# Keys and queries with tokens on the partitions, roots by token block, and a changed order of the attention loop

## Chip, cores and metric

One core of a Trainium2 chip. The time is device microseconds of one execution of the whole program; smaller is better. Engines: TensorE (PE, with its weight loads PEld), VectorE (DVE), ScalarE (ACT), GpSimd (POOL), and SyncE (SP), which issues the DMAs.

## The reference, cut to what matters

256 tokens of width 1024 pass two blocks in float32: six gated feed-forward networks, a mixer of four parts, a gated linear recurrence, and attention at the end. The change touches the keys and values, which come from one projection of the normalised activations, and the queries of the attention:

```python
def shared_kv(x, kv_gain, w_kv, k_gain):
    hkv = rms_norm_2(x, kv_gain)
    k, v = jnp.split(hkv @ w_kv, 2, axis=-1)
    return rms_norm_2(heads(k), k_gain), heads(v)          # 16 heads of 64

def stick_breaking_block(h, k, v, w_q, q_gain, w_o):
    q = rms_norm_2(heads(h @ w_q), q_gain)
    o = stick_breaking_attention(q, k, v)                   # two blocks of 128 queries
    ...
    # z = q k / 8;  w[t, s] = sigmoid(z[t, s]) * prod over s' in (s, t) of sigmoid(-z[t, s']);  o = w v
```

`rms_norm_2` divides by the root of the mean square plus 1e-6 and multiplies by a gain. Keys and queries are thus normalised twice: the input over 1024 features of a token, the result over the 64 features of a head.

## The kernel before, in words

Activations lie with features on the partitions: `x` is 128 x 8 tiles x 256 tokens. Every float32 weight block (128 x 1024, 512 KB) is loaded by SP into one of six slots of `raw`; ACT copies it to `w_hi` in the type fp32r (`hi`, L652), and POOL, or DVE for some blocks, subtracts that from `raw` and gives `w_lo` (`lo`, L557, L1072). The activations are cut likewise into a high and a low half (`xn`, and `kv_in` for the keys and values). A product is then three: high by high, high by low, low by high. All engines go through the blocks in one order; a slot is free for `raw` after `lo_ready`, and for `w_hi` after `used`, which TensorE raises at a block's last product.

The stages that matter are `kv` (8 blocks of keys `split_in`, 8 of values `split_rows`), the feed-forward `ffn_e`, then `q_in` (8 blocks `split_in`), the attention, and `attn_out` (8 blocks of rows, the first two used in float32 without cutting).

Keys and queries before: `projections` makes a tile of 128 output features by 256 tokens at a time, with the weights loaded into the array and 256 tokens moving (`head_tiles`, L1861 to L1863). The first four tiles run together, input tile by input tile, and `total_squares` (L1893) sums the squares of x over the features in between. DVE multiplies each tile by `rstd` out of PSUM (`take`, L1278), ACT squares two tiles at a time (L957).

- For the keys, a product with `head_ones` (L2378, 128x512) sums the squares over the features of a head, ACT takes the root (L962), DVE the reciprocal of 128x512 (L1702) and the scaled product (L1703). The values have tokens on the partitions (`rows_tile`, L1958 to L1960: tokens loaded, 512 weight columns moving) and need `rstd` as a column: four records of L2389.
- For the queries, the squares are summed with tokens on the partitions (`token_squares`, L2415), ACT takes roots of 8 or 16 columns (L990), DVE their reciprocals (L1746), and `over_features` (L2427) spreads them over 64 partitions each by products with the identity; DVE then scales (L1751).

The attention loop runs over eight pairs of heads `c`. For each: `logits` on PE (L2441 to L2447) into banks 0 to 3, two sigmoids on ACT (L1008), a recurrence along the keys (L1767) and the product that gives the weights on DVE (L1771), six transposes on PE into banks 4 and 5 (L2499), their copy by ACT (L1024), `weighted_values` on PE (L2459 to L2463), and their copy to `y` (L1013). `rows(0)` and `rows(1)` (L1923) start the output projection in float32; they write banks 0 to 3, and so wait for the last sigmoids. `unused_products(2)` are two products (L2474) whose result is not used.

Each engine's instructions run in the order written. The waits are on counters: `need(engine, name, value)` waits until the counter has that value.

## Time and profile before

| | us |
|---|---|
| median of 3 runs | 1542.15 (1541.9 to 1542.18) |
| the profiled execution, time | 1542.68 |
| the profiled execution, span | 1540.5 |
| PE busy | 1526.4 (99%) |
| DVE busy | 1070.8 (70%) |
| POOL busy | 925.2 (60%) |
| ACT busy | 777.9 (50%) |
| chain that ended last, PE | 92% |
| HBM read, mean | 261 MB, 170 GB/s |
| granted TensorE clock, tenths | 9, the highest digit, in all 40 slices |

The busy time of PE is from each matmul's start to its modelled end, and these overlap: what one costs in a full stream is the distance between the starts of neighbours. In a timeline row the first number is the start from the span's beginning, the second the length, and `xN` the number of records merged into the row. A float32 matmul leaves two records, one in fp32r or a transpose leaves one. Where an engine idled before a row, the row says for how long and what ended it.

### The profile page before, as it was taken

How to read it: one execution, taken by the hardware profiler on the slowest of the kernel's cores; microseconds unless marked ns; L12 is line 12 of the kernel's file. 1: busy time of each engine (PE TensorE's matmuls, PEld its weight loads, DVE VectorE, ACT ScalarE, POOL GpSimd, SP SyncE). 2: the span in 40 equal slices, each digit the busy share in tenths (PEclk: the TensorE clock that was granted, in tenths of full speed). 3: DMA queues.
4: the chain of work that ended last, by engine and by line, in shares of the span. 5: the costliest groups of instructions: out<-in, count | busy, mean ns of one | idle time of the engine just before them, and what ended most of it. 6: DMA issues, size and time to landing. Idle time of an engine off the chain costs nothing.

```text
span 1540.5 us, 25103 instructions
## 1 busy us (share of the span) xinstructions
PE 1526.4 (99%) x9754; PEld 1332.9 (87%) x9754; DVE 1070.8 (70%) x1475; ACT 777.9 (50%) x1119; POOL 925.2 (60%) x1092
## 2 busy tenths in 40 slices
PE   9999999999999999999999999999999999999998
PEld 7888888887888888888999888888888889888887
DVE  7866555765976668976589976657866655697664
ACT  6554432023654565554666654555555455665542
POOL 4966520201686677876776686677967671167663
PEclk9999999999999999999999999999999999999999
DMA  8666533232656565665635566564565562346653
GB/s 299 207 198 182 192 110 110 70 97 83 204 197 194 164 200 163 198 199 183 200 124 186 182 197 194 165 225 145 179 201 180 171 221 67 125 164 204 184 162 119
DMA packets 107350, 263.69 MB, mean 171 GB/s; under 512 B 9184, under 2 KB 43104, under 8 KB 107104
## 3 DMA queue, kind: packets, MB, share of 16 engines
q1 hardware_dynamic: 107232, 262.09, 52.5%
q8 instruction: 78, 1.28, 0.3%
q14 instruction: 40, 0.33, 0.1%
HBM read 261.00 MB, written 1.05 MB: 170 GB/s over the span
## 4 chain that ended last, share of the span: by engine, by line
PE 92%; DVE 5%; ACT 1%; DMA 1%; issue 1%; POOL 0%; SPq 0%; DVEq 0%; ACTq 0%
PE ps L1827 42%; PE ps L1828 24%; PE ps L1877 6%; PE ps L1830 5%; PE ps L1923 2%; PE ps L1861 2%; PE ps L1863 2%; PE ps L1862 2%; PE ps L1944 1%; PE ps L2135 1%; DMA raw<-blocks 1%; PE ps L2030 1%; DVE arena L1767 1%; PE ps L1960 0%; PE ps L1958 0%
## 5 line engine op out<-in xcount | busy, mean ns | idle before, releaser
L557 POOL TENSOR_TENSOR w_lo<-raw,w_hi 128x256 fp32r<-128x256 f32 x1056 | 904.4, 889 | 494.9 <-ACT w_hi L652 491.2
L1827 PE MATMUL ps<-xn,w_hi 128*128 128x512 f32 x1848 | 660.1, 396 | 1.3 <-DVE xn L1083 0.7
L652 ACT ACTIVATE w_hi<-raw 128x1024 fp32r<-128x1024 f32 (+1 forms) x517 | 476.8, 933 | 187.3 <-PE ps L1830 104.3
L1828 PE MATMUL ps<-xn,w_lo 128*128 128x256 f32 x2112 | 550.4, 280 | 0.0
L1827 PEld LDWEIGHTS ps<-xn,w_hi 128*128 128x128 f32 x1848 | 346.5, 187 | 77.9 <-DVE xn L1083 1.4
L1828 PEld LDWEIGHTS ps<-xn,w_lo 128*128 128x128 f32 x2112 | 398.4, 189 | 17.4
L1827 PE MATMUL ps<-hid,w_hi 128*128 128x512 f32 x1008 | 363.5, 397 | 0.0
L1072 DVE TENSOR_TENSOR w_lo<-raw,w_hi 128x512 fp32r<-128x512 f32 (+1 forms) x246 | 285.8, 1163 | 39.2 <-ACT w_hi L652 34.2
L1828 PE MATMUL ps<-hid,w_lo 128*128 128x256 f32 x1056 | 292.5, 282 | 0.0
L1827 PEld LDWEIGHTS ps<-hid,w_hi 128*128 128x128 f32 x1008 | 190.2, 189 | 41.0
L1178 DVE TENSOR_TENSOR arena<-ps,low_part 128x512 f32<-128x512 f32 x132 | 90.8, 688 | 191.6 <-ACT low_part L767 191.4
L1828 PEld LDWEIGHTS ps<-hid,w_lo 128*128 128x128 f32 x1056 | 198.5, 188 | 7.5
L767 ACT ACTIVATE low_part<-ps 128x512 f32<-128x512 f32 x132 | 78.3, 593 | 172.6 <-PE ps L1830 172.5
L772 ACT ACTIVATE arena<-arena 128x256 f32<-128x256 f32 x132 | 55.3, 419 | 147.0 <-DVE arena L1188 147.0
L1188 DVE TENSOR_TENSOR arena<-arena,rstd 128x512 f32<-128x512 f32 x132 | 111.8, 847 | 4.5
L1830 PE MATMUL ps<-xn,w_hi 128*128 128x512 f32 x264 | 104.1, 396 | 0.0
L1877 PE MATMUL ps<-xs,raw 128*128 128x256 f32 x432 | 98.3, 382 | 0.0
L1198 DVE TENSOR_TENSOR h<-arena 128x256 f32<-128x256 f32 x132 | 93.2, 706 | 0.0
L1877 PEld LDWEIGHTS ps<-xs,raw 128*128 128x128 f32 x432 | 80.7, 190 | 12.2 <-issue 1.1
L1199 DVE TENSOR_TENSOR hid<-h,hid 128x256 fp32r<-128x256 f32 x132 | 86.6, 656 | 4.5
L1197 DVE TENSOR_TENSOR hid<-arena 128x256 fp32r<-128x256 f32 x132 | 61.2, 464 | 29.1 <-ACT arena L772 29.1
L1220 DVE SCALAR_TENSOR_TENSOR x<-ps,x 128x512 f32<-128x512 f32 x24 | 16.5, 686 | 73.1 <-PE ps L1830 73.1
(342 smaller groups left out, 1490.3 us busy)
## 6 DMA issues: line engine op xcount, KB each, us to landing
raw<-blocks SPq DMA_DIRECT2D x418, 512.0 KB, 3.6
raw<-blocks SPq DMA_DIRECT2D x146, 256.0 KB, 3.5
cst<-consts SPq DMA_DIRECT2D x1, 2358.0 KB, 14.3
x<-x_in SPq DMA_DIRECT2D x4, 256.0 KB, 5.5
out<-x SPq DMA_DIRECT2D x4, 256.0 KB, 3.3
cst<-consts SPq DMA_DIRECT2D x1, 109.0 KB, 2.1
```

Of the source, the lines that this page charges most:

```text
L557: ins = nc.gpsimd.tensor_tensor(w_lo[:, slot(n), piece], raw[:, slot(n), piece], w_hi[:, slot(n), piece], ALU.subtract)
L652: nc.scalar.activation(w_hi[:, slot(n), cols], raw[:, slot(n), cols], ACT.Copy)\
L767: nc.scalar.activation(low_part[:, :, :], ps[:, b:b + 2, SEQ:], ACT.Copy).then_inc(low_taken, 1)
L1072: nc.vector.tensor_tensor(w_lo[:, slot(n), cols], raw[:, slot(n), cols], w_hi[:, slot(n), cols], ALU.subtract).then_inc(lo_ready[slot(n)], 1)
L1178: nc.vector.tensor_tensor(gate_up[:, :, :], ps[:, b:b + 2, 0:SEQ], low_part[:, :, :], ALU.add)\
L1188: nc.vector.tensor_tensor(gate_up[:, :, :], gate_up[:, :, :], over(rstd[:, :], 2), ALU.mult)\
L1198: chain(nc.vector.tensor_tensor(h[:, :], gate_up[:, 1, :], gs, ALU.mult))
L1199: nc.vector.tensor_tensor(hid[:, c, 1, :], h[:, :], hid[:, c, 0, :], ALU.subtract)\
L1827: nc.tensor.matmul(where, hi, both.rearrange("p a t -> p (a t)"), start=opens, stop=False)
L1828: ins = nc.tensor.matmul(where[:, 0:SEQ], lo, high, start=False, stop=False)
L1830: ins = nc.tensor.matmul(where, hi, both.rearrange("p a t -> p (a t)"), start=False, stop=True)
L1877: ins = nc.tensor.matmul(where, raw[:, slot(n), k * P:k * P + P], xs[:, k, :], start=k == 0, stop=k == KD - 1)
```

## The change

The 16 blocks of key and query weights are loaded in another cut (`split_cols`): a block holds two input tiles for four output tiles, in four pieces of 256 columns. `token_steps` loads 128 tokens of the activations into the array and moves 512 weight columns, two input tiles a block; the first half (output tiles 0 to 3) is complete before the second, in banks 4 and 5, then 6 and 7. The norm over the 1024 features is not applied to keys and queries: since q/rstd cancels under the second norm but for epsilon, the mean square of a head gets the bias 1e-6 times (mean square of x plus 1e-6), `heads_eps`. Per half `u` (0 and 1 keys, 2 and 3 queries) and block of 128 tokens `t`: ACT squares 128x512 out of PSUM, DVE sums groups of 64 (`tensor_reduce`), ACT takes 8 roots, DVE 8 reciprocals and the product 128x512, PE turns it with four transposes (`turn`) in the same bank, and ACT or DVE copy it with the gain into `k_t` or `q_t`. `total_squares` is replaced in these stages by `token_totals`, after step 7 of 8 of the first half; `rstd` over features is kept for `ffn_e` alone. `head_ones` products, `token_squares`, `over_features`, the column products and `unused_products` go. In the loop the sigmoids of pair 2 stand ahead of the first copy of weights, and the row tiles 0 to 7 of `rows(0)` come as (0, 1), (2, 3, 4), (5, 6, 7), the first two before the transposes of pair 6; they were (0 to 3) after its values and (4 to 7) after the transposes of pair 7.

```diff
--- before.py
+++ after.py
@@ -116,9 +116,9 @@
...
-    add("kv", ["split_in"] * 8 + ["split_rows"] * 8)
+    add("kv", ["split_cols"] * 8 + ["split_rows"] * 8)
...
-    add("q_in", ["split_in"] * 8)
+    add("q_in", ["split_cols"] * 8)
...
+        def token_bank(half, t):
+
+            return 4 + 2 * half + t
+
+        def token_tiles(b):
+
+            return ps[:, b, :].rearrange("p (o m) -> p o m", m=P)
...
+                elif KINDS[n] == "split_cols":
+                    start, cols = h0 + 4 * (at // 4), slice(PAIR * (at % 4), PAIR * (at % 4) + PAIR)
+                    sp.dma_start(raw[:, slot(n), :].rearrange("p (o m) -> p o m", m=PAIR),
+                                 blocks[start:start + 4, :, cols].rearrange("o p m -> p o m")).then_inc(arrived[slot(n)], 16)
...
+                if gains in TOKEN_NORMS:
+                    return
...
+            def heads_square(u, n0):
+
+                last = n0 + 4 * (u % 2) + 3
+                act.wait_ge(used[slot(last)], nth(last))
+                for t in range(TB):
+                    nc.scalar.activation(sq_heads[2 * (u % 2) + t], ps[:, token_bank(u % 2, t), :], ACT.Square)\
+                        .then_inc(ev["heads_sq"], 1)
+
+            def heads_root(u):
+                for t in range(TB):
+                    need(act, "heads_sums", 2 * u + t + 1)
+                    nc.scalar.activation(heads_inv[:, u % 2, t, :], heads_inv[:, u % 2, t, :], ACT.Sqrt, scale=1.0 / HD,
+                                         bias=heads_eps[:, t:t + 1]).then_inc(ev["heads_root"], 1)
+
+            def heads_take(u, t, dst, by):
+
+                need(act, "heads_turned", 2 * u + t + 1)
+                half = u % 2
+                nc.scalar.activation(dst[:, 4 * half:4 * half + 4, t * P:t * P + P], token_tiles(token_bank(half, t)), ACT.Copy,
+                                     scale=const(by)).then_inc(ev["heads_ready"], 1)
...
-                for a in range(4):
-                    heads_square(1, a)
-                    hi_until(n0 + 9 + a)
-                for a in range(4):
-                    heads_root(1, a)
-                    hi_until(n0 + 13 + a)
+                act.wait_ge(total_ready, state["norms"])
+                nc.scalar.activation(rstd_col[:, :], ps[:, 3, SEQ:SEQ + TB], ACT.Sqrt, scale=1.0 / D, bias=const("norm_eps"))
+                nc.scalar.activation(rms[:, :], ps[:, 3, 0:SEQ], ACT.Sqrt, scale=1.0 / D, bias=const("norm_eps"))\
+                    .then_inc(rms_ready, 1)
+                heads_square(0, n0)
+                hi_until(n0 + 9)
+                heads_root(0)
+                hi_until(n0 + 12)
+                for t in range(TB):
+                    heads_take(0, t, k_t, "k_norm")
+                hi_until(n0 + 13)
+                heads_square(1, n0)
+                hi_until(n0 + 14)
+                heads_root(1)
+                hi_until(n0 + 16)
+                for t in range(TB):
+                    heads_take(1, t, k_t, "k_norm")
                 hi_until(n0 + 2 * KD + 4)
                 act.wait_ge(used[slot(n0 + 2 * KD - 1)], nth(n0 + 2 * KD - 1))
-                need(act, "col_out", 1)
+                act.wait_ge(rstd_ready, state["norms"])
                 for t in range(TB):
                     ins = nc.scalar.activation(v_heads[:, t, :], ps[:, 2 * t:2 * t + 2, :].rearrange("p b s -> p (b s)"),
                                                ACT.Copy, scale=rstd_col[:, t:t + 1])
                 ins.then_inc(ev["v_out"], 1)
...
+                n0, out_rows = FIRST["q_in"], FIRST["attn_out"]
+                hi_until(n0 + KD - 1)
+                heads_square(2, n0)
+                heads_root(2)
                 preload(ACT.Sigmoid)
                 need(act, "at_mask", 1)
...
+                def take_weights(c):
                     need(act, "at_wt", c + 1)
                     nc.scalar.activation(weights_t[c % 2][:, :, :].rearrange("p (b m) s -> p b (m s)", b=2),
                                          ps[:, 4:6, 0:3 * P], ACT.Copy).then_inc(ev["at_wt_out"], 1)
+
+                heads_take(2, 0, q_t, "q_norm")
+                sigmoids(0)
+                sigmoids(1)
+                preload(ACT.Sqrt)
+                heads_square(3, n0)
+                heads_root(3)
+                preload(ACT.Sigmoid)
+                sigmoids(2)
+                take_weights(0)
+                heads_take(3, 0, q_t, "q_norm")
+                for c in range(1, KD):
+                    if c + 2 < KD:
+                        sigmoids(c + 2)
+                    take_weights(c)
                     if c == KD - 1:
                         hi_until(out_rows + 4)
-                    if c:
-                        output(c - 1)
+                    output(c - 1)
                     if c == KD - 2:
                         hi_until(out_rows + 3)
...
+                if gains and gains not in TOKEN_NORMS:
                     inverse_root(gains)
+
+            def token_norm(gains):
+
+                norms[0] += 1
+                v.wait_ge(total_ready, norms[0])
+                return nc.vector.tensor_scalar(heads_eps[:, :], ps[:, 3, SEQ:SEQ + TB], NORM_EPS / D, NORM_EPS * NORM_EPS, ALU.mult, ALU.add)
...
+            def heads_sums(u):
+
+                for t in range(TB):
+                    need(v, "heads_sq", 2 * u + t + 1)
+                    signal(nc.vector.tensor_reduce(heads_inv[:, u % 2, t, :], sq_heads[2 * (u % 2) + t].rearrange("p (g s) -> p g s", s=HD),
+                                                   axis=mybir.AxisListType.X, op=ALU.add), "heads_sums")
+
+            def heads_unit(u):
+
+                half = u % 2
+                for t in range(TB):
+                    inv = heads_inv[:, half, t, :]
+                    need(v, "heads_root", 2 * u + t + 1)
+                    chain(nc.vector.reciprocal(inv, inv))
+                    by = heads_inv[:, half, t, :].unsqueeze(2).broadcast_to([P, 8, HD])
+                    signal(tt(heads_tok[:, t, HALF * half:HALF * half + HALF].rearrange("p (g s) -> p g s", s=HD),
+                              ps[:, token_bank(half, t), :].rearrange("p (g s) -> p g s", s=HD), by, ALU.mult), "heads_unit")
+
+            def heads_take(u, t, dst, by):
+
+                need(v, "heads_turned", 2 * u + t + 1)
+                half = u % 2
+                tsc(dst[:, 4 * half:4 * half + 4, t * P:t * P + P], token_tiles(token_bank(half, t)), const(by), None, ALU.mult)\
+                    .then_inc(ev["heads_ready"], 1)
...
-                heads_take(n0, 0)
-                heads_take(n0, 1)
                 for a in range(4):
                     low_halves("g_ffn_e", a)
+                roots[0] += 1
+                v.wait_ge(rms_ready, roots[0])
+                chain(token_norm("g_kv"))
+                nc.vector.reciprocal(rstd_col[:, :], rstd_col[:, :]).then_inc(rstd_ready, 1)
+                heads_sums(0)
+                heads_unit(0)
+                chain(nc.vector.reciprocal(rstd[:, :], rms[:, :]))
                 lo(n0 + 9)
-
-                need(v, "col_done", 1)
-                signal(nc.vector.tensor_copy(rstd_col[:, :], ps[:, 3, 0:TB]), "col_out")
-                heads_take(n0, 2)
-                heads_take(n0, 3)
+                heads_sums(1)
+                heads_unit(1)
                 lo(n0 + 13)
-                for a in range(4):
-                    heads_finish(1, a, k_t, "k_norm")
...
+                token_norm("g_attn").then_inc(rstd_ready, 1)
+                v.wait_ge(rstd_ready, norms[0])
+                heads_sums(2)
+                heads_unit(2)
+                heads_take(2, 1, q_t, "q_norm")
                 for c in range(KD):
-                    if c == 1:
-                        take_query(7)
-                        scaled_queries(2)
+                    if c == 2:
+                        heads_sums(3)
+                        heads_unit(3)
+                        heads_take(3, 1, q_t, "q_norm")
...
+            def token_totals(over_features=False):
+
+                norms[0] += 1
+                pe.wait_ge(sum_ready, norms[0])
+                if over_features:
+                    mm(ps[:, 3, 0:SEQ], const("all_ones"), squares_sum[:, 0:SEQ], start=True, stop=True)
+                for t in range(TB):
+                    ins = mm(ps[:, 3, SEQ + t:SEQ + t + 1], squares_sum[:, t * P:t * P + P], const("all_ones")[:, 0:1], start=True, stop=True)
+                ins.then_inc(total_ready, 1)
+
+            def token_steps(n0, halves, half, steps, after_norm=None):
+
+                for k in steps:
+                    n = n0 + 4 * half + k // 2
+                    if after_norm is not None:
+                        pe.wait_ge(xn_lo_ready, KD * SPLIT_NORMS.index(after_norm) + k + 1)
+                    if k % 2 == 0:
+                        pe.wait_ge(lo_ready[slot(n)], nth_split(n))
+                    wh, wl = (w[:, slot(n), :].rearrange("p (o k m) -> p k o m", k=2, m=P)[:, k % 2] for w in (w_hi, w_lo))
+                    for t in range(TB):
+                        where, tok = token_tiles(token_bank(half, t)), slice(t * P, t * P + P)
+                        mm(where, halves[:, k, 0, tok], wh, start=k == 0, stop=False)
+                        mm(where, halves[:, k, 0, tok], wl, start=False, stop=False)
+                        ins = mm(where, halves[:, k, 1, tok], wh, start=False, stop=k == KD - 1)
+                    if k % 2:
+                        ins.then_inc(used[slot(n)], 1)
+
+            def turn(u, t):
+
+                need(pe, "heads_unit", 2 * u + t + 1)
+                half = u % 2
+                for i in range(4):
+                    at = HALF * half + i * P
+                    ins = nc.tensor.transpose(ps[:, token_bank(half, t), i * P:i * P + P], heads_tok[:, t, at:at + P], const("ident"))
+                ins.then_inc(ev["heads_turned"], 1)
...
+                token_steps(n0, kv_in, 0, range(7), "g_kv")
+                token_totals(over_features=True)
+                token_steps(n0, kv_in, 0, (7,), "g_kv")
+                token_steps(n0, kv_in, 1, range(6))
+                turn(0, 0)
+                turn(0, 1)
+                token_steps(n0, kv_in, 1, (6, 7))
                 pe.wait_ge(rstd_ready, norms[0])
-                for t in range(TB):
-                    ins = mm(ps[:, 3, t:t + 1], rstd[0:1, t * P:t * P + P], const("all_ones")[0:1, 0:1], start=True, stop=True)
-                ins.then_inc(ev["col_done"], 1)
-                tile(2)
-                need(pe, "col_out", 1)
-
-                need(pe, "proj_out", before + 6)
                 for k in range(KD):
                     rows_tile(n0 + KD + k, kv_in[:, k, :, :], start=k == 0, stop=k == KD - 1)
-                    if 1 <= k < 5:
-
-                        need(pe, "proj_out", before + KD)
-                        heads_squares(1, k - 1)
+                    if k == 2:
+                        turn(1, 0)
+                        turn(1, 1)
+                need(pe, "heads_ready", 4)
...
-                    if c == 0:
-                        need(pe, "proj_out", before + 6)
+                    need(pe, "heads_ready", 6 if c < 4 else 8)
                     if c == 1:
-                        need(pe, "q_root", 2)
+                        pe.wait_ge(rstd_ready, norms[0])
                     if c >= 2:
                         need(pe, "at_sig", c - 1)
...
                     if c < 2:
-                        need(pe, "heads_ready", 4 + 3 + c)
+                        need(pe, "heads_ready", 8)
...
+                token_steps(n0, xn, 0, range(7), "g_attn")
+                token_totals()
+                token_steps(n0, xn, 0, (7,), "g_attn")
+                token_steps(n0, xn, 1, range(3))
+                turn(2, 0)
+                turn(2, 1)
+                token_steps(n0, xn, 1, (3,))
+                logits(0)
+                token_steps(n0, xn, 1, (4,))
+                logits(1)
+                token_steps(n0, xn, 1, (5, 6, 7))
+                logits(2)
+                turn_weights(0)
+                logits(3)
+                turn(3, 0)
+                turn(3, 1)
+                for c in range(1, KD):
+                    if c == KD - 2:
+                        rows(0, (0, 1))
+                    turn_weights(c)
+                    if c == KD - 1:
+                        rows(0, (5, 6, 7))
+                    weighted_values(c - 1)
+                    if c == KD - 2:
+                        rows(0, (2, 3, 4))
                     if c == 1:
-                        over_features(3)
-                    if c == KD - 1:
-                        rows(0, range(4, KD))
-                    if c:
-                        weighted_values(c - 1)
-                    if c == KD - 2:
-                        rows(0, range(4))
+                        logits(4)
                     if c + 4 < KD:
                         logits(c + 4)
                 rows(1, range(4))
```

## Rows read from the trace of the kernel before

**Rows 1.** The page's first part: busy time, share of the span, instructions.
```profile
PE 1526.4 (99%) x9754; PEld 1332.9 (87%) x9754; DVE 1070.8 (70%) x1475; ACT 777.9 (50%) x1119; POOL 925.2 (60%) x1092
```

**Rows 2.** Timeline of PE, key-and-value stage: start us, us, engine, line, operation, shape, count.
```profile
1033.32 0.28 PE L1861 MATMUL ps<-kv_in,w_hi 128*128 128x256 f32 x1
...
1039.07 0.59 PE L1893 MATMUL ps<-arena,cst 128*128 128x256 f32 x2
...
1039.62 0.28 PE L1862 MATMUL ps<-kv_in,w_hi 128*128 128x256 f32 x1
...
1062.97 1.02 PE L2378 MATMUL ps<-arena,cst 128*128 128x512 f32 x2
...
1064.06 0.40 PE L1959 MATMUL ps<-w_lo,kv_in 128*128 128x512 f32 x1
...
1076.03 0.39 PE L1958 MATMUL ps<-w_hi,kv_in 128*128 128x512 f32 x1
...
1082.83 0.39 PE L1827 MATMUL ps<-xn,w_hi 128*128 128x512 f32 x1
```

**Rows 3.** Timeline of PE, query projection with its sums and spreads.
```profile
1274.17 0.59 PE L1893 MATMUL ps<-arena,cst 128*128 128x256 f32 x2
...
1283.23 1.84 PE L2415 MATMUL ps<-cst,arena 128*128 128x2 f32 x16
...
1285.14 0.28 PE L1862 MATMUL ps<-xn,w_hi 128*128 128x256 f32 x1
...
1287.98 1.97 PE L2427 MATMUL ps<-cst,q_inv 128*64 128x128 f32 x32
...
1290.10 0.28 PE L1862 MATMUL ps<-xn,w_hi 128*128 128x256 f32 x1
```

**Rows 4.** Timeline of PE, logits, turned weights, values and row tiles.
```profile
1295.01 0.70 PE L2441 MATMUL ps<-arena 64*128 64x256 f32 x4
...
1296.21 0.28 PE L1861 MATMUL ps<-xn,w_hi 128*128 128x256 f32 x1
...
1324.80 0.82 PE L2499 MATMUL ps<-cst,arena 128*128 128x128 f32 x6
1325.46 1.89 PE L1923 MATMUL ps<-y,raw 128*128 128x256 f32 x8
1327.28 0.44 PE L2459 MATMUL ps<-arena 128*64 128x128 f32 x4
...
1328.09 1.99 PE L1923 MATMUL ps<-y,raw 128*128 128x256 f32 x8
```

**Rows 5.** Windows: stretch, its length, busy us of each engine, granted clock, DMA.
```profile
1057.50:1082.80 25.30, 25.30 (x106) 19.55 (x105) 17.25 (x9) 12.03 (x14) 20.35 (x28) 1.00 0.53 177
1268.40:1304.70 36.30, 36.03 (x320) 34.28 (x319) 20.68 (x38) 17.12 (x26) 9.28 (x14) 1.00 0.28 84
1304.70:1325.50 20.80, 18.61 (x186) 15.35 (x185) 18.11 (x14) 18.11 (x27) 0.00 (x0) 1.00 0.01 2
```

**Rows 6.** Timeline of ACT, attention: a table load, two pairs' sigmoids, one copy of weights.
```profile
1294.12 1.28 ACT L663 ACT_TABLE_LOAD   x1
...
1295.65 2.92 ACT L1008 ACTIVATE arena<-ps 128x768 f32<-128x768 f32 x4
...
1305.93 0.82 ACT L1024 ACTIVATE arena<-ps 128x768 f32<-128x768 f32 x1
```

**Rows 7.** Timeline of DVE: reciprocal, two-input sum, small reciprocal, recurrence, weights.
```profile
1066.91 3.35 DVE L1702 RECIPROCAL arena<-arena 128x512 f32<-128x512 f32 x1
...
1272.69 0.68 DVE L1095 TENSOR_TENSOR arena<-arena,xs 128x512 f32<-128x512 f32 x1
...
1294.20 0.20 DVE L1746 RECIPROCAL q_inv<-q_inv 128x8 f32<-128x8 f32 x1 [0.66 <-ACT q_inv L990]
...
1315.73 1.77 DVE L1767 TENSOR_TENSOR_SCAN arena<-arena 128x774 f32<-128x774 f32 x1
1317.54 0.96 DVE L1771 TENSOR_TENSOR arena<-arena 128x768 f32<-128x768 f32 x1
```

## What the change should do to the time

> **What bounds the kernel now.** Read the page's first part first: TensorE is busy in 99% of the span [rows 1]. In such a kernel a microsecond counts only if it is TensorE's, as work or as idle time. Then the timeline of PE, where the distance of starts gives the real price of a product. In the key stage 48 products of 256 columns lie between 1033.32 and 1039.07: 0.120 us each. From 1076.03 to 1082.83 there are 30 products of 512 columns: 0.227 each [rows 2]. Last the windows, for idle time. In the query stage PE misses 0.27 us of 36.30, and in the loop 2.19 of 20.80 [rows 5], so there a second bound is close. DVE's recurrence starts at 1315.73, its weights product at 1317.54 for 0.96 us, and the next recurrence follows at about 1318.53 [rows 7]: 2.8 us a pair, back to back.
>
> **The key stage.** It runs from 1033.32 to 1082.83, 49.5 us [rows 2]. Its parts:
> - 192 products of 256 columns at 0.120: 23.0. After: 96 of 512 at 0.227, 21.8. Columns are equal, seams are fewer.
> - Totals: 1039.62 less 1039.07 less one product of 0.12, 0.43. After: the same 0.43 and two products of one moving column. Eight such products (16 records) took 1285.14 − 1283.23 − 0.12 = 1.79 [rows 3], 0.22 each; together 0.87.
> - Values, 96 of 512 columns: 21.8, before and after.
> - Four `head_ones` products: 1064.06 − 1062.97 − 0.23 = 0.86 each [rows 2], 3.4. They go.
> - The rest, 49.5 − 23.0 − 0.43 − 21.8 − 3.4 = 0.9, is the column products and seams; I keep 0.3 of it.
> - New: 16 transposes. Six took 1325.46 − 1324.80 = 0.66 [rows 4], 0.11 each, 1.8.
>
> After: 21.8 + 0.87 + 21.8 + 1.8 + 0.3 = 46.6, **2.9 us less**, if nothing waits. Count from the stage's start. Half 0 ends at 11.8. ACT still has the halves for `ffn_e` and two roots in front of its squares and starts them about 13.3; I take 0.68 for each 128x512 operation on ACT or DVE (the sum of two inputs, [rows 7]) and 0.20 for each one on 8 columns (the small reciprocal, [rows 7]). Squares, sums, one copy of a weight block, roots and products come to about 18; the turn stands at 19.9. For half 1: squares from 24, product done by about 30, turn at about 31.7. Both have some 2 us to spare. The moves on the queues: on ACT, squares, roots and takes stand ahead of later `hi` copies, so `w_hi` of the next blocks, then POOL's low halves, then SP's loads, queue behind them. But blocks now come free one by one (each 12 x 0.227 = 2.7 us) where four were released together, and ACT stands idle over half of the value stretch, POOL 5 of 25 us [rows 5]. DVE loses four reciprocals of 3.35 us there [rows 7]. I cost the queues at nothing; should cover fail, one copy of about 1 us stands ahead of a block.
>
> **The query stage and the loop.** The start is 1274.17 less 48 x 0.12 = 1268.42 [rows 3]; all times from here count from it. The last transposes (pair 7) start at 1324.80, that is 56.4 [rows 4]. TensorE's work loses 1.2 in the projection, 32 records of `token_squares` (2 x 1.79 = 3.6), 64 of `over_features` (2 x (1290.10 − 1287.98 − 0.12) = 4.0 [rows 3]) and two unused products (2 x 0.43); it gains 1.8 of transposes: 7.9 net. Whether that reaches the end depends on the chains of ACT and DVE, so I lay the order out:
> - PE: seven steps of 6 x 0.227 = 1.36 to 9.5, totals to 10.0, half 0 done at 11.3, three more steps to 15.4.
> - ACT squares 11.6 to 12.9; DVE sums to 13.7, products done at 14.5 and 15.4. `turn(2, 0)` at 15.4 is just met, `turn(2, 1)` at 15.9 too. ACT's table load of 1.28 [rows 6] fits before the take at 16.1. Copies done at 17.2.
> - Logits 0 at 17.7, at 1.2 each (1295.01 to 1296.21 [rows 4]), a step, logits 1, three steps to 25.7. ACT's sigmoids, 2.92 / 4 = 0.73 each [rows 6], give pair 0 at 20.7, pair 1 at 23.2; DVE's weights are ready at 23.6 and 26.4.
> - PE goes on: logits 2 to 26.9, transposes 0, logits 3 to 29.0. ACT loads the root table and squares from 25.9 to 27.3; DVE sums, behind its second weights, to 28.0; products at 28.9 and 29.8. `turn(3, 1)` waits about 0.4, done at 30.4.
> - ACT: table load, sigmoids 2 from 29.8 to 31.3, copy of weights 0 (0.82 [rows 6]) to 32.1. The transposes of pair 1 need banks 4 and 5 and wait for that copy: a **new stall of 1.7 us**, behind it on PE the values and logits 4 and 5.
> - DVE: recurrence 2 from 31.4 (37.7 before); six pairs of 2.8 end at 48.3, the last sigmoids at 45.4. PE's first two row tiles wait for these (about 0.6 idle), then 2 x 0.43 (eight records of L1923 from 1325.46 to 1327.28 are four tiles, 0.45 each), transposes 0.7, values 0.8 (1327.28 to 1328.09 [rows 4]), three tiles 1.3: transposes 7 at 49.1.
>
> Before they stood at 56.4 with four tiles done, now at 49.1 with five: 7.3 + 0.45 = **7.7 us less**. The tail behind (rows, values, `output_rows`) is unchanged on PE, and its `hi` and `lo` of output blocks keep their distance. Bounds: if the stalls vanished, DVE would still allow transposes 7 at 47.4 at the earliest, a gain of 9.4. For `tensor_reduce` of 128x512 no row exists; below lies 0.2 (eight elements), above 3.35 (the slowest DVE operation on that shape [rows 7]). I take 0.68, the other one-pass operation. The moving operand in four runs has no row either: the ends are 0.227, all in one run, and 0.43 for 256 columns in float32; I take 0.227, since nothing but the addresses differs from the value stretch.
>
> A page speaks against the sums on DVE: by the Trainium skill, VectorE: DVE Perf Modes, section Rules for kernel authors, a tensor_reduce on the hot path never leaves the single-rate mode and is called the slowest operation; its table's single-rate float32 figure, scaled to 512 columns, is an estimate of 0.57 us, with which the sum stays as it is. On the strided weights the Trainium skill, SBUF — State Buffer, section Door 1: The DMA port swizzle, charges each step to a new 16-byte line, and runs of 128 floats touch as many lines as one run does; by that the price is the contiguous one.
>
> **Sum.** 2.9 + 7.7 = 10.6 from the profiled execution's 1542.68 gives 1532.1; that execution lies 0.5 above the median, so 1531.5 as a median.
>
> **The rivals.**
> - *The gain is partly turned into waits* (chance 0.17): the turns are met with only 0.1 to 0.4 us, and each 0.3 more on a square, sum or product delays both query halves and the loop behind. Two units late by 1 us each, and 1 to 2 us more where copies wait on ACT: 3 to 5 us lost, 1534.5 to 1537. For it: the tight turns, and ACT and DVE each busy 18.1 of 20.8 us in the loop [rows 5]. Against: DVE waits in the query stage (20.7 busy of 36.3).
> - *The moving operand in four runs is slower* (0.04): the place is `token_steps`, 192 products; each 0.1 us more costs 19 us. It decides from 10.6 / 192 = 0.055, that is at 0.28 a product. At the float32 end, 0.86 for 512 columns, it would be 120 us; at 0.34, midway to the 0.45 of half rate, 1553. Slower. Against: the float32 columns of the head are read in the same way from the same array.
> - *A slow sum over groups* (0.03): at 3.35 each, two sums stand in each query half, 5 us late twice, and the key turns miss their 2 us by 3 twice: 10 to 16 lost of the 10.6 gained, 1541.5 to 1547: no change or slower.
> - *The clock is granted lower* (0.02): with stalls of 1.7 us and many transposes PE might fall to 1.2 GHz; 10 us of such work would cost 10, so no change. Against: 1.00 in the loop, with 2.19 us idle [rows 5].
> - *Nothing of it happens* (0.02): the stages keep their length because transposes in a bank just read, or loads in 1 KB pieces, hold PE; 1542.
>
> My forecast has 0.72. **Predicted 1531.5 us.** The range takes in the vanished stalls (9.4 + 2.9 = 12.3, 1529.8, and a little for the seams) and the first rival: 1529 to 1537. About 0.2% (3 us) is what a measurement can tell from no change; faster by that 0.90, within it 0.05, slower 0.05.
>
> **What would show it.** L1861 to L1863 gone from both stages and in their place 512-column products at 0.227; the key stage 46.6 long; transposes 7 at 49 from the query start; PE idle near 1.7 before the transposes of pair 1, released by ACT's copy; recurrences 2 to 7 back to back at 2.8. A distance above 0.25 in the new products, or a PE wait over 1 us at a turn for DVE, would make the prediction wrong.

## The result, and the profile after

The changed kernel takes 1532.16 us (median of 4 runs, 1531.4 to 1533.08) against 1542.16 before (1541.9 to 1542.41): ratio 0.9935, interval 0.9918 to 0.9953. It is faster by 0.65%, and the prediction of 1531.5 is 0.7 us off. The profiled execution took 1531.62, with a span of 1529.6; the span before was 1540.5, so the traces differ by 10.9 us.

The first part of the page of the changed kernel (share of the span and instructions; beside [rows 1], 10.2 us of TensorE's work and 266 matmul records are gone):

```profile
span 1529.6 us, 24560 instructions
PE 1516.2 (99%) x9488; PEld 1316.1 (86%) x9488; DVE 1047.1 (68%) x1471; ACT 779.6 (51%) x1127; POOL 919.8 (60%) x1092
```

Its PE timeline in the key stage, from the first key product to the first product of `ffn_e` (start, length, line, shapes, records):

```profile
1032.93 0.40 PE L2428 MATMUL ps<-w_hi,kv_in 128*128 128x512 f32 x1
...
1049.77 0.39 PE L2429 MATMUL ps<-w_lo,kv_in 128*128 128x512 f32 x1
...
1052.71 0.39 PE L2430 MATMUL ps<-w_hi,kv_in 128*128 128x512 f32 x1
1052.94 1.03 PE L2440 MATMUL ps<-cst,arena 128*128 128x128 f32 x8
1053.73 0.48 PE L2428 MATMUL ps<-w_hi,kv_in 128*128 128x512 f32 x1
...
1064.73 1.03 PE L2440 MATMUL ps<-cst,arena 128*128 128x128 f32 x8
1065.52 0.48 PE L1992 MATMUL ps<-w_hi,kv_in 128*128 128x512 f32 x1
...
1079.23 0.39 PE L1861 MATMUL ps<-xn,w_hi 128*128 128x512 f32 x1
```

L2428 to L2430 are the new products, with 512 weight columns moving; L2440 is the turn of keys or queries. From 1049.77 to 1052.71 there are 13 products, 0.226 us each. Each eight transposes cost 0.79 to 0.80 (1052.94 to 1053.73), without a wait before them. The stage lasts 1079.23 − 1032.93 = 46.30; it was 49.51 [rows 2].

DVE in the changed kernel, the keys' first half (L1739 sums over groups, L1748 small reciprocals, L1750 scaled products):

```profile
1046.23 1.39 DVE L1739 TENSOR_REDUCE heads_inv<-arena 128x8 f32<-128x512 f32 x2
1047.65 0.20 DVE L1748 RECIPROCAL heads_inv<-heads_inv 128x8 f32<-128x8 f32 x1
1047.89 0.69 DVE L1750 TENSOR_TENSOR arena<-ps,heads_inv 128x512 f32<-128x512 f32 x1
...
1048.85 0.69 DVE L1750 TENSOR_TENSOR arena<-ps,heads_inv 128x512 f32<-128x512 f32 x1
```

Two sums take 1.39, 0.70 each, about as much as the scaled product beside them. The products are done at 1049.54; the turn that reads them stands at 1052.94, so 3.4 us are in hand.

PE in the changed kernel, from the query stage's first product to the end of the loop. L2508 are the six transposes of a pair's weights, L1957 the row tiles (two records a tile):

```profile
1264.83 0.40 PE L2428 MATMUL ps<-w_hi,xn 128*128 128x512 f32 x1
...
1295.00 0.66 PE L2440 MATMUL ps<-cst,arena 128*128 128x128 f32 x4 [0.31 <-DVE arena L1750]
1297.26 0.85 PE L2508 MATMUL ps<-cst,arena 128*128 128x128 f32 x6 [1.60 <-ACT arena L1045]
...
1308.65 0.85 PE L2508 MATMUL ps<-cst,arena 128*128 128x128 f32 x6 [0.18 <-ACT arena L1045]
...
1310.36 1.13 PE L1957 MATMUL ps<-y,raw 128*128 128x256 f32 x4
...
1312.89 1.56 PE L1957 MATMUL ps<-y,raw 128*128 128x256 f32 x6
1314.29 0.82 PE L2508 MATMUL ps<-cst,arena 128*128 128x128 f32 x6
...
1339.08 0.50 PE L1861 MATMUL ps<-xn,w_hi 128*128 128x512 f32 x1
```

From here on times count from the query stage's first product. The turn of the last queries waits 0.31 us. The transposes of pair 1 wait 1.60 us, released by L1045, ACT's copy of weights 0: the predicted new stall. The transposes of pair 7 start at 49.46, with five tiles in front of them; before at 56.38 with four [rows 3, 4]. The first product of `ffn_f` (the last row) comes at 74.25; before it came at 81.61, so the query stage with all up to `ffn_f` is 7.36 shorter.

ACT in the changed kernel, ahead of that stall (L982 roots, L677 the table of the sigmoids, L1036 sigmoids of pair 2, L1045 the copy):

```profile
1293.05 0.30 ACT L982 ACTIVATE heads_inv<-heads_inv,heads_eps 128x8 f32<-128x8 f32 x1 [0.42 <-DVE heads_inv L1739]
1293.37 1.28 ACT L677 ACT_TABLE_LOAD   x1
1294.66 0.20 ACT L677 ACTIVATE table<-table 1x4 f32<-1x4 f32 x1
1294.90 1.51 ACT L1036 ACTIVATE arena<-ps 128x768 f32<-128x768 f32 x2
1296.30 0.82 ACT L1045 ACTIVATE arena<-ps 128x768 f32<-128x768 f32 x1
```

ACT is busy from 1293.05 to the end of the copy at 1297.12: root, table, sigmoids and copy run one after the other, and PE, idle from 1295.66, waits for the last of them. The windows of the changed kernel (busy us of PE, PEld, DVE, ACT, POOL, then the clock) show how full the loop is:

```profile
1264.83:1294.00 29.17, 29.17 (x155) 23.39 (x153) 20.70 (x35) 16.58 (x26) 10.25 (x14) 1.00 0.30 104
1294.00:1316.00 22.00, 19.86 (x178) 15.97 (x178) 19.52 (x17) 20.14 (x32) 0.00 (x0) 1.00 0.01 2
1316.00:1339.10 23.10, 23.10 (x187) 21.58 (x186) 12.79 (x17) 13.03 (x21) 6.80 (x8) 1.00 0.65 242
```

The idle time of PE in the query stage, 2.14 us, all lies in the middle window; it was 0.27 + 2.19 before [rows 5], and nothing behind these windows. So of the 7.36 us, 7.04 are removed work and 0.32 less idling, and the stall of 1.60 took the place of waits that were there already. The balance of the two traces: 3.21 + 7.36 = 10.57, and 0.39 from an earlier start of the key stage; together 10.96 of 10.9. The 0.39 is no part of the change: TensorE's code in front is the same in all kernels, and over the profiles of this document the stage starts anywhere from 1032.35 to 1033.73. `ffn_e`, between the two stages, lasts 185.60 after and 185.59 before.

### The profile page after: what moved, and what is told of

Same layout as the page of the kernel before. It is cut to its first block, busy times and chain, and to the rows that moved or that the text cites. A ratio compares the mean times of both kernels' runs of the same rounds, so it can differ in the third digit from the quotient of the medians.

```text
span 1529.6 us, 24560 instructions
## 1 busy us (share of the span) xinstructions
PE 1516.2 (99%) x9488; PEld 1316.1 (86%) x9488; DVE 1047.1 (68%) x1471; ACT 779.6 (51%) x1127; POOL 919.8 (60%) x1092
## 3 DMA queue, kind: packets, MB, share of 16 engines
q8 instruction: 75, 1.23, 0.3%
## 4 chain that ended last, share of the span: by engine, by line
PE 92%; DVE 4%; ACT 1%; DMA 1%; issue 1%; POOL 0%; SPq 0%; DVEq 0%; ACTq 0%
PE ps L1861 42%; PE ps L1862 24%; PE ps L1911 6%; PE ps L1864 5%; PE ps L1957 2%; PE ps L1978 1%; PE ps L2428 1%; PE ps L2430 1%; PE ps L2429 1%; PE ps L2169 1%; PE ps L2064 1%; DMA raw<-blocks 1%; PE ps L1897 1%; PE ps L1896 1%; PE ps L1895 1%
```

## The experiments

Every kernel is a variant of the changed one. "Key stage", "transposes 7" and "to `ffn_f`" are read as above: 46.30, 49.46 and 74.25 in the changed kernel; 49.51, 56.38 and 81.61 before.

**The keys alone.** The queries are computed and normalised as before, and the attention loop has its old order (the diff shows a part of the edit).

```diff
-    add("q_in", ["split_cols"] * 8)
+    add("q_in", ["split_in"] * 8)
...
-TOKEN_NORMS = ("g_kv", "g_attn")
+TOKEN_NORMS = ("g_kv",)
...
-                heads_square(2, n0)
-                heads_root(2)
+                pair_square(0)
+                pair_square(1)
+                token_roots(0, 1)
+                pair_square(2)
+                token_roots(2, 2)
```

> The key-and-value stage is as in the changed kernel, the query stage and the attention loop are those of before. Theory (two independent gains): about 3.2 us below the kernel before (49.5 us less the 46.3 that the trace of the changed kernel shows for this stage), 1539.0, and a ratio near 0.998; the key stage 46.3 long in the trace, the time from the query start to the transposes of pair 7 again 56.4. Rival (the two stages share a resource, for instance POOL's lead at ffn_e, so that the key stage alone gives other than its share): under 1.5 or over 5 us. On the spread of the changed kernel's times (1531.4 to 1533.1, mean granted clock 0.998 in the slower ones): if the attention's new order brings it, this kernel's times lie within 0.5 us and its clocks are 1.000; if the key stage brings it, they spread by 1.5.

Measured: 1538.63 (11 runs, 1538.14 to 1539.37) against 1541.87 (15 runs), ratio 0.9978, interval 0.9969 to 0.9987. Key stage 46.30, transposes 7 at 56.25, to `ffn_f` 81.48. The last sentence of the expectation was not met on either side: the times spread by 1.23 us and yet all granted clocks are 0.999 or 1.000. The 15 times of the kernel before spread by 1.56 us, with the same clocks. So a spread of this size is no sign of the clock by itself.

**The changed kernel again**, on the same chip, unedited.

> The changed kernel once more, nothing edited. Theory: 1531.4 to 1533.1 as before, ratio 0.993 to 0.994; the slower times are those with a mean granted clock below 1.000, 0.75 us for each 0.001 (half clock over 1.5 us). Rival (the spread is another thing): times and clocks are not in one order.

Measured: 1531.65 (1531.23, 1531.61, 1531.65, 1532.64, 1532.66), ratio 0.9935, interval 0.9922 to 0.9947. So the two parts come apart on one chip: the keys give 1541.87 − 1538.63 = 3.24, the queries with the new order of the loop 1538.63 − 1531.65 = 6.98. The traces say 3.21 and 7.36. The five times fall into two groups 1 us apart; what that is comes below. The price in the expectation is too low by half: 0.001 of the mean clock is 1.5 us of a span of 1530, not 0.75.

**Weights in one run.** The moving operand of `token_steps` is read in one run of 512 instead of four of 128. The kernel leaves out the choice of the right columns: its keys and queries are other numbers, with products of the same count and shape.

```diff
-                    wh, wl = (w[:, slot(n), :].rearrange("p (o k m) -> p k o m", k=2, m=P)[:, k % 2] for w in (w_hi, w_lo))
+                    wh, wl = (w[:, slot(n), HALF * (k % 2):HALF * (k % 2) + HALF] for w in (w_hi, w_lo))
...
-                        where, tok = token_tiles(token_bank(half, t)), slice(t * P, t * P + P)
+                        where, tok = ps[:, token_bank(half, t), :], slice(t * P, t * P + P)
```

> token_steps reads its 512 weight columns as one run of the block in place of four runs of 128; keys and queries are then other numbers. Theory (four runs cost nothing): 0.227 us a product as in the changed kernel, and the time is unchanged within 0.5 us. Rival (each jump of address costs a few ns that the modelled ends hide): below 0.225 a product, and 192 products give 1 us or more.

Measured: 1531.57; key stage 46.3, transposes 7 at 49.46, to `ffn_f` 74.25, all as in the changed kernel. Its PE groups of the keys' products (records, busy us, mean ns):

```profile
L2428 PE MATMUL ps<-w_hi,kv_in 128*128 128x512 f32 x32 | 12.7, 396 | 0.0
L2430 PE MATMUL ps<-w_hi,kv_in 128*128 128x512 f32 x32 | 12.5, 390 | 0.0
L2429 PE MATMUL ps<-w_lo,kv_in 128*128 128x512 f32 x32 | 12.5, 390 | 0.0
```

The changed kernel's groups of the same lines have the same numbers, 396, 390 and 390 ns. Four runs cost nothing that these traces show; that rival is excluded, not only unlikely.

**Sums of the queries' first half twice.** The spare time of the query turns, priced: one more `tensor_reduce` for each token block of `heads_sums(2)`.

```diff
                     need(v, "heads_sq", 2 * u + t + 1)
+                    for _ in range(1 if u in (2,) else 0):
+                        chain(nc.vector.tensor_reduce(heads_inv[:, u % 2, t, :], ...))
```

> Each of the two sums over groups of the first query half is done twice (0.7 us more each), result unchanged. Theory (the first query turn has 0.1 to 0.3 us of slack, and what is behind it is shifted whole): PE waits about 1.2 us before the second block's turn, and transposes 7 stand 1.1 to 1.3 us later from the query start, 50.7. Rival (slack downstream, the 1.6 us stall before the transposes of pair 1, swallows it): transposes 7 stay within 0.4 us of 49.5 and that stall shrinks.

Measured: 1533.43 (span 1531.5), transposes 0 of the loop at 28.35 instead of 27.11, transposes 7 at 50.70, to `ffn_f` 75.49. Its PE timeline at the two query turns:

```profile
1281.67 0.66 PE L2443 MATMUL ps<-cst,arena 128*128 128x128 f32 x4 [0.51 <-DVE arena L1753]
1282.63 0.66 PE L2443 MATMUL ps<-cst,arena 128*128 128x128 f32 x4 [0.30 <-DVE arena L1753]
```

About 1.4 us of added DVE work arrive as 1.24 us at the end, as expected, but the wait is not the one of 1.2 us that was expected: it is 0.51 before the first turn and 0.30 before the second, the rest longer distances beside them. The query turns have almost nothing in hand, as the layout said ("just met"), and nothing behind absorbs it: the stall before the transposes of pair 1 is 1.61 here too.

**Sums of the keys four times.**

```diff
                     need(v, "heads_sq", 2 * u + t + 1)
+                    for _ in range(3 if u in (0, 1) else 0):
+                        chain(nc.vector.tensor_reduce(heads_inv[:, u % 2, t, :], ...))
```

> Each sum over groups of the keys is done four times (three more of 0.7 us, 4.2 us more in each half), result unchanged. In the changed kernel the products of the keys are done 3.4 us and 1.9 us ahead of the end of their turns' natural start. Theory (slack is what the trace shows, and only the excess costs): the first half's second turn waits about 0.45 us, the second half's about 0.8, the key stage is 47.4 to 47.8 long in place of 46.3, the query stage is unchanged. Rival (DVE's delayed low halves of blocks 9 and 13, or SP's loads behind them, hold PE too): a wait of PE for w_lo or a key stage over 49.

Measured: 1534.46 (span 1532.6), key stage 47.92. That is 0.12 above the expected range. Its PE timeline shows waits at the key turns, for DVE's products (idle before, in brackets):

```profile
1053.79 0.66 PE L2443 MATMUL ps<-cst,arena 128*128 128x128 f32 x4 [0.31 <-DVE arena L1753]
...
1065.62 0.66 PE L2443 MATMUL ps<-cst,arena 128*128 128x128 f32 x4 [0.27 <-DVE arena L1753]
1066.59 0.66 PE L2443 MATMUL ps<-cst,arena 128*128 128x128 f32 x4 [0.30 <-DVE arena L1753]
```

Six added sums of 0.70, 4.2 us of DVE a half, cost the key stage 1.62 in all: 0.88 in these three waits, the rest in longer distances around them (the four transposes from 1052.83 to 1053.79, without their wait, take 0.65 where four in a full stream take 0.40). So most of the added work was absorbed: the slack of 3.4 and 1.9 us at the turns was real. By it, one more sum a block (1.4 us a half) should have been free in the key stage, where it cost 1.24 in the query stage; that kernel was not run.

This trace had something that I had not expected of it: to `ffn_f` 75.73, 1.48 more, in a stage that the edit does not touch. One of its windows (columns as above; clock after the five engines):

```profile
1298.50:1302.00 3.50, 3.25 (x20) 2.62 (x22) 3.43 (x3) 3.00 (x6) 0.00 (x0) 0.51 0.01 2
```

From 1298.5 to 1302.0 the granted clock is 0.51 on average, the level of 1.2 GHz; cut finer, it is 0.50 from 1298.6 to 1302.0 and 1.00 on both sides. The fall begins within the stall of pair 1, on this kernel's PE timeline 1.61 us:

```profile
1298.75 1.51 PE L2511 MATMUL ps<-cst,arena 128*128 128x128 f32 x6 [1.61 <-ACT arena L1045]
1300.19 0.70 PE L2492 MATMUL ps<-arena 128*64 128x128 f32 x4
```

Six transposes take 1.51 where they took 0.85. In the trace of the changed kernel, with the same stall, the clock stayed at 1.00. This looked like the second group of times; the runs after it are about the stall.

**The copy in front of the sigmoids.** ACT takes weights 0 before the sigmoids of pair 2, the order of before.

```diff
-                sigmoids(2)
                 take_weights(0)
+                sigmoids(2)
```

> One part of the change undone: the first weights' copy stands ahead of the third pair's sigmoids on ACT. Theory (ACT is full here, so the order only moves the stall): the wait of 1.6 us before the transposes of pair 1 goes, PE waits about 1.4 us before the values of pair 0 instead, for ACT's take of the last queries; recurrence 2 starts 0.8 us later; transposes 7 at 49.4 to 49.8 from the query start (49.46 now). Rival 1 (the copy was what mattered): transposes 7 at 48.3 or less. Rival 2 (DVE's chain is the bound, so 0.8 us later is 0.8 us lost): 50.2.

Measured: 1531.55 (span 1529.7), transposes 1 at 31.02 (1.41 sooner), transposes 7 at 49.35 (a little before the 49.4 to 49.8 expected), to `ffn_f` 74.15. On its PE timeline the stall did not go away, it is now behind those transposes, where `weighted_values(0)` waits for the take of the last queries that the sigmoids push back:

```profile
1296.03 0.85 PE L2508 MATMUL ps<-cst,arena 128*128 128x128 f32 x6 [0.20 <-ACT arena L1045]
1298.01 0.44 PE L2489 MATMUL ps<-arena 128*64 128x128 f32 x4 [1.13 <-ACT arena L989]
```

Whichever comes first on ACT, PE waits for the other: 1.4 us less at one place give 0.10 at the end. Putting the sigmoids in front, as the change does, is worth nothing by itself; by this trace it costs 0.10 us.

**The copy between the two roots.** ACT waits 0.42 us for DVE between its two roots (the bracket in the ACT rows above); the copy goes there.

```diff
-            def heads_root(u):
+            def heads_root(u, between=None):
                 for t in range(TB):
+                    if t and between:
+                        between()
...
-                heads_root(3)
+                heads_root(3, between=lambda: take_weights(0))
                 preload(ACT.Sigmoid)
                 sigmoids(2)
-                take_weights(0)
```

> The first weights' copy stands between the two roots of the second query half on ACT, where ACT waits 0.4 us for a sum. Theory: second root, turn (3, 1) and recurrence 2 are 0.6 us later, the stall before the transposes of pair 1 goes, and the values of pair 0 start at 33.0 in place of 33.2: transposes 7 at 49.2 to 49.5. Rival 1: 48.3 or less, the stall was a net loss. Rival 2: 50.0, DVE bounds.

Measured: 1530.54 (span 1528.6), transposes 1 at 30.67, transposes 7 at 49.10 (49.2 to 49.5 expected), to `ffn_f` 73.89, 0.36 sooner. The query stage started 0.59 sooner than in the changed kernel, in front of the edit, so of the 1.0 us between the two spans only 0.36 belongs to it. ACT of this kernel (L1047 is the copy):

```profile
1291.74 0.30 ACT L984 ACTIVATE heads_inv<-heads_inv,heads_eps 128x8 f32<-128x8 f32 x1 [0.33 <-DVE heads_inv L1740]
1292.21 0.81 ACT L1047 ACTIVATE arena<-ps 128x768 f32<-128x768 f32 x1 [0.17 <-PE ps L2509]
1292.92 0.29 ACT L984 ACTIVATE heads_inv<-heads_inv,heads_eps 128x8 f32<-128x8 f32 x1
```

The roots are 1.18 apart instead of 0.72, so of the copy's 0.81 only 0.46 lies on ACT's chain; behind it the chain has one operation less. PE's largest idle stretch in the loop is 1.26 now, before the values of pair 0.

**The two row tiles where they were.**

```diff
-                    if c == KD - 2:
-                        rows(0, (0, 1))
...
-                        rows(0, (5, 6, 7))
+                        rows(0, range(4, KD))
...
-                        rows(0, (2, 3, 4))
+                        rows(0, range(4))
```

> One part undone: row tiles 0 to 3 behind the values of pair 5, 4 to 7 behind the transposes of pair 7, as before the change. Theory (PE is dense here, tiles only change places): transposes 7 start 0.2 to 0.4 us earlier with one tile of 0.45 fewer behind them, and the distance from the query start to ffn_f is 74.3 to 74.5 (74.25 now): the part is worth 0.1 to 0.2 us. Rival (the two early tiles fill a real gap): 74.9 or more.

Measured: 1531.62 (span 1529.8), but that kernel started its query stage 0.55 sooner than the changed one, so the time hides the effect. Transposes 7 come at 49.75 (with four tiles), to `ffn_f` 74.97, 0.72 later. PE waits where the tiles stood:

```profile
1308.11 0.85 PE L2508 MATMUL ps<-cst,arena 128*128 128x128 f32 x6 [0.18 <-ACT arena L1045]
...
1310.61 0.85 PE L2508 MATMUL ps<-cst,arena 128*128 128x128 f32 x6 [0.85 <-ACT arena L1045]
```

My theory missed here: 74.3 to 74.5 was expected, and the rival's 74.9 or more came. I expected that the gap would be small; it is 0.85 us, and the two tiles of the change fill it with 0.97 us of work that has to be done anyway. Of the two reorderings tested, this one pays.

**Copy between the roots, timed.** The same kernel as above, with five rounds, beside the next three on one chip (before: 1542.2, 9 runs, 1541.31 to 1542.75).

> The kernel with the first weights' copy between the two roots, timed in rounds. Of this chip's clock the last runs showed: in one execution, of keys_sums, the granted clock was 0.50 from about 1298.5 to 1302, from the end of the 1.6 us stall on, and the pair behind it took 1.5 us longer; executions of the changed kernel fall into two groups, near 1531.5 and near 1532.7. Theory (the stall brings the fall in some executions): without it this kernel has one group, no execution with a clock under 0.999 and the higher time, median 1530.8 to 1531.2, ratio 0.9928 to 0.9932. Rival (the fall comes from elsewhere): two groups here too, 1.2 us apart.

Measured: 1530.68 (1530.65, 1530.66, 1530.68, 1530.99, 1531.35), ratio 0.9926, interval 0.9913 to 0.9938. It has the lowest median of all kernels. Its times lie together, within 0.70 us, and so do those of the long stall below; those of the other two kernels of this series fall into two groups. Its profile has 73.90 to `ffn_f`, as the first one (73.89), and no clock below 1.00 in the loop.

**The changed kernel, timed a third time.**

> The changed kernel, unedited, beside it. Theory: two groups 1.2 to 1.5 us apart, each with at least one execution of five. Rival: one group, and then the comparison says nothing.

Measured: 1533.14 (1531.28, 1532.97, 1533.14, 1533.15, 1533.17), ratio 0.9938, interval 0.9925 to 0.995. Its profile fell on a long execution (span 1531.2). The windows of PE alone (length, busy us, clock):

```profile
1294.84:1298.30 3.46, 1.69 (x14) 0.98 0.00 0
1298.30:1301.80 3.50, 3.50 (x24) 0.53 0.02 5
1301.80:1338.84 37.04, 36.81 (x312) 1.00 0.37 133
```

The stall before transposes 1 is 1.60, as in the first profile, transposes 1 come at 32.43 as there. Cut finer, the clock is 0.50 from 1298.2 to 1301.6; here it falls 0.9 us after the stall is over. To `ffn_f` 75.81, 1.56 more. That is about the difference of the two groups of spans: 1529.3 to 1529.7 and 1530.7 to 1531.2. Of the 2.46 us between the medians of this kernel and of the copy between the roots, then, some 1.5 are the clock and 0.36 the order; most of the rest lies in front of the query stage (it starts at 1264.84 in this profile and at 1264.31 in the other kernel's).

**A longer stall.** Two more table loads ahead of the sigmoids of pair 2.

```diff
                 preload(ACT.Sigmoid)
+                preload(ACT.Sqrt)
+                preload(ACT.Sigmoid)
                 sigmoids(2)
```

> Two further table loads on ACT (1.5 us each with its dummy) ahead of the third pair's sigmoids: the stall before the transposes of pair 1 grows from 1.6 to 4.6 us, result unchanged. Theory (a longer idle time makes the fall certain): the profile shows 0.50 for a few us behind the stall; all executions together, 3.0 for the stall and 1.5 or more for the clock above 1531.5: 1536.0 or more. Rival (the stall alone does not bring it): clock 1.00 behind the stall and 1534.5.

Measured: 1536.95 (five runs, 1536.72 to 1537.28), ratio 0.9965, interval 0.9951 to 0.9978. PE's timeline and windows:

```profile
1300.66 1.52 PE L2510 MATMUL ps<-cst,arena 128*128 128x128 f32 x6 [4.64 <-ACT arena L1045]
```

```profile
1295.97:1300.60 4.63, 0.06 (x1) 0.82 0.00 0
1300.60:1305.30 4.70, 4.63 (x27) 0.50 0.00 0
```

To `ffn_f` 79.61, 5.36 more: 3.04 of longer stall (4.64 − 1.60), and 2.32 of the clock. All five times lie together. The clock falls already within the stall (0.82 over its window): cut finer, it is 0.50 from 1298.9 to 1305.7, twice as long as in the other falls. About 5 us of that lie behind the stall; their half would be 2.5.

**The stall cut in two.** `turn_weights(0)` is followed by the two turns, and logits 3 stand between them and the transposes of pair 1.

```diff
                 turn_weights(0)
-                logits(3)
                 turn(3, 0)
                 turn(3, 1)
+                logits(3)
```

> logits 3 stand behind the turns of the second query half: PE's idle time of 0.3 and 1.6 us becomes about 1.2 before turn (3, 0), 0.4 before turn (3, 1) and 0.7 before the transposes of pair 1; all else, the start of these transposes at 32.4 and of transposes 7 at 49.5 included, stays. Theory (it is the long single gap that brings the fall): one group near 1531.5. Rival (the sum of idle time in the stretch counts): two groups as in the changed kernel.

Measured: 1531.57 (1530.58, 1531.38, 1531.57, 1533.02, 1533.39), ratio 0.9933, interval 0.9921 to 0.9945. The profiled one is the longest (span 1531.5). Its PE timeline, and its windows:

```profile
1294.83 0.66 PE L2440 MATMUL ps<-cst,arena 128*128 128x128 f32 x4 [1.27 <-DVE arena L1750]
1295.79 0.66 PE L2440 MATMUL ps<-cst,arena 128*128 128x128 f32 x4 [0.30 <-DVE arena L1750]
...
1298.06 1.51 PE L2508 MATMUL ps<-cst,arena 128*128 128x128 f32 x6
```

```profile
1265.62:1296.30 30.68, 29.10 (x153) 1.00 0.27 99
1296.30:1299.80 3.50, 3.50 (x22) 0.59 0.00 0
```

No idle stretch is longer than 1.27 us, and the clock fell all the same; cut finer, it is 0.50 from 1297.0 to 1300.4 (the window above starts too early). The slow logits 3 fill the 0.7 us of idle time that were expected before the transposes of pair 1, so to `ffn_f` it is 75.32, only 1.07 more than without a fall. Two groups of times came, as the rival said, and the theory that it is the single stall of 1.6 us that counts does not hold as such.

## Why the prediction was right, and where it was not

The median lay 0.7 us above the forecast, well inside the range, and the mechanism was the one forecast: less work on TensorE in both stages, with one new stall. That the sum came so close, 10.6 forecast and 10.57 measured over the two stages, is in part luck: the key stage gave 0.3 more than forecast and the query stage 0.3 less, and within the query stage two misses of more than half a microsecond worked against each other. By its steps:

- **Key stage**: 46.6 forecast, 46.30 measured. Products at 0.226 to 0.227, transposes at 0.10 each (0.79 for eight, where I took 0.11), no waits. The queues, costed at nothing, were nothing: in the keys-alone run the stage is 46.30 too and gives 3.24 us of time. "Both have some 2 us to spare": 3.4 and 1.95.
- **Query stage**: 7.7 less forecast, 7.36 measured in the trace, 6.98 between medians of one chip. The removed work was priced too high, 7.9 net forecast against 7.04 measured (the stage less its idle time: 81.61 − 2.46 = 79.15 before, 74.25 − 2.14 = 72.11 after): a part of it is that the product behind a turn or the totals takes 0.32 to the next start where the sum has 0.227 (1053.73 to 1054.05, likewise in the query stage). The idle time was priced too high as well, 0.4 + 1.7 + 0.6 = 2.7 against 2.14: of the 0.6 before the first two row tiles nearly nothing came. The order of events came as laid out: recurrence 2 at 31.6 (1296.44 in DVE's timeline; 31.4 forecast), then six at 2.8, transposes 7 at 49.46 (49.1). The miss of 0.36 was made before transposes 1 (32.43 for 32.1), and from there on both run 17.0 us. About 0.2 of it is the projection itself (the transposes of pair 0 stand at 27.11, where the layout had 26.9), and 0.1 the small root in ACT's chain, taken at 0.20 from DVE's reciprocal on 8 columns, 0.30 on ACT.
- **The new stall**: 1.7 forecast, 1.60 to 1.61 measured, released by the copy as said. The wait at `turn(3, 1)`: 0.4 forecast, 0.31.
- **`tensor_reduce`**: taken at 0.68, measured 0.70. The estimate of 0.57 from the Trainium skill's VectorE: DVE Perf Modes was lower than both, and what its section Rules for kernel authors calls it, the slowest operation, is not borne out here: the two-input product on the same shape takes 0.69, and the reciprocal takes 3.35 [rows 7].
- **Four runs**: taken at the contiguous price; the one-run kernel shows that it is.
- **The rival that the gain turns into waits** did not come, but the query-sums run shows its mechanism and price: 1.24 us of delay for about 1.4 us of DVE work. Its condition, sums or squares longer by 0.3 or more, is what was not met: the sums were 0.02 above the forecast, and a pair of squares took 1.06 to 1.09 where twice 0.68 was taken.
- **The rival of the clock** was weighed wrongly. I gave it 0.02, for a stretch of 10 us, and argued that 2.19 us of idle time in the old loop had not moved the clock. But these lay in pieces, the longest of them this one:

```profile
1321.35 0.88 PE L2499 MATMUL ps<-cst,arena 128*128 128x128 f32 x6 [1.11 <-DVE arena L1771]
```

And the fall is not of the kernel but of an execution. The three series of the changed kernel have 14 executions; by their spans 8 are in the upper group, an estimate, as only one of the 8 was profiled and other kernels spread by 1.2 to 1.6 us without such a fall in their profiles. It costs 1.56 us in the one that was profiled, not 10. It explains why the median of the first series, 1532.16, lies between its runs of 1531.4 and 1533.08. The right term in the sum would have been "0 or 1.5, about as often as not", and that such a term was left out is part of the 0.7 us.
- **The reorderings**, which I counted together with the rest, come apart: the sigmoids in front of the copy 0.10 us against (copy in front: 74.15), and the two tiles 0.72 for (74.97 without). Each is read from one trace; three traces of kernels in which nothing changes there have 74.25 all.

What stays open is when the clock falls. Seen at 0.50 for 3.4 us: one profile of the changed kernel out of three, the keys with four sums, the split stall, and, for 6.8 us, the long stall, whose five times agree. Where it begins differs: 0.2 us before the stall's end, 0.9 after it, and 1.2 after the last of the idle pieces in the split one, so no fixed distance from the stall sets it. Not seen: the other two profiles of the changed kernel, the one-run, query-sums and late-tiles kernels with the same stall of 1.60 to 1.61, the copy in front of the sigmoids (0.30, 0.20 and 1.13 us idle, one execution), and the copy between the roots, which has 0.30 us idle, 1.3 us of work, and 1.26 idle: none of its 6 executions is in an upper group, where 2 of the 5 of the split stall are, with 1.27, 0.66 of work, 0.30. With these counts the difference between the last two can be chance. That the copy between the roots avoids the fall is what the runs suggest, not what they show; that its gain of 0.36 is real, its two traces without a fall show (73.89 and 73.90).

## What to carry to other kernels

When TensorE bounds a kernel at 99%, write down the removed work in distances of starts, then lay out the other engines' chains with the new order and see which wait stands where: here that gave 10.6 us forecast and 10.57 measured in the trace. Removed work arrives in full only up to the next dependency, so price the slack of each turn; here 1.4 us more on DVE cost 1.24 where nothing was in hand, and 8.4 us more cost 1.62 where 3.4 and 1.9 were. An idle stretch of TensorE may cost more than its length, in some executions, through the clock, as the stall of 1.6 us did here: if times of one kernel fall into two groups, look at the granted clock behind its longest stall. And when moving one instruction only moves a stall, look for idle time on the engine that is waited for: a copy placed partly in 0.42 us of idle ACT time gained 0.36 us, more than either order of copy and sigmoids.

## What the runs showed of the hardware

- With a stall of 1.6 us TensorE's granted clock can fall to 0.50 for 3.4 us, in one execution and not in another of the same kernel: six transposes 1.51 instead of 0.85, four value products 0.70 instead of 0.44, 1.5 us lost in all. It was seen in 2 of the 7 profiles with this stall. With a stall of 4.64 us it was 0.50 for 6.8 us, and the five times of the kernel agree with a fall in each.
- A float32 moving operand of the fp32r type in four runs of 128 is read as fast as one run of 512: 390 to 396 ns a record in both, 0.226 between starts.
- ACT's root of 128x8 with a bias per partition takes 0.30 us. By the Trainium skill, ScalarE: Activation LUTs, section What ACT_TABLE_LOAD costs, an activation with such a bias has a fixed part of about 280 ns and 0.833 ns an element, an estimate of 0.29 for 8 columns; the row agrees, and it would have been the better price for the forecast than DVE's reciprocal.
